# First attention stage: pooled projections first, separate operands for the pooled and convolved channels, two output chunks in each late step

## The reference, cut to what matters

```python
h = modulate(rmsnorm(x, g_mix), sh1, sc1)
proj = h @ w_in                       # q, k, v: 512 each; u_pool, b_gate, c_gate, x_conv: 256 each
attn = diff_attention(q, k, v, ...)   # 8 heads, two softmaxes each, over 512 x 512
y_a = rmsnorm(attn, g_subln) * 0.8                       # 512 channels
y_b = multiscale_pool(u_pool, w_pool, pool_scale)        # 256: window means less the token, a 64x64 map, a scale
y_c = b_gate * conv3(c_gate * x_conv)                    # 256
mixed = concatenate([y_a, y_b, y_c]) @ w_out
x = x + gt1 * mixed
```

## Time and profile before

| what | value |
|---|---|
| median of 3 runs | 1758.97 us |
| the profiled execution | 1761.21 us, its span 1759.4 us |
| TensorE matmul busy | 1699.7 us, 97% of the span |
| VectorE, ScalarE, GpSimd busy | 822.9, 618.2, 139.6 us |
| mean granted clock of TensorE | 0.984 |
| the 17 steps of the first attention | about 74.6 to 235.3 us |
| first addition to x of the attention's own output chunks | 258.33 us |

### The profile page before, as it was taken

One profiled execution on the slowest core, in us unless ns is written; L12 is line 12 of the kernel. 1 busy time (PEld: TensorE's weight loads), 2 busy tenths in 40 slices (PEclk: granted clock), 3 DMA queues, 4 the chain that ended last, 5 costly groups with the idle time before them and its releaser, 6 DMA issues.

```text
span 1759.4 us, 22619 instructions
## 1 busy us (share of the span) xinstructions
PE 1699.7 (97%) x7999; PEld 1367.6 (78%) x7999; DVE 822.9 (47%) x1272; ACT 618.2 (35%) x1071; POOL 139.6 (8%) x142
## 2 busy tenths in 40 slices
PE   5999998999999999999999999999999999999998
PEld 3866576888888888888888887677788888888886
DVE  4788756443333334444444434666455544444332
ACT  4365534222222323322222221555443322223222
POOL 0002101000001113000001030002001100000000
PEclk8999898999999999999999999999999999999998
DMA  9543113443333326333343346122233333333331
GB/s 344 194 133 114 42 54 94 141 131 95 95 100 99 98 85 151 95 95 95 95 118 99 94 126 116 50 59 70 72 95 95 90 99 98 96 95 109 99 98 64
DMA packets 296590, 184.55 MB, mean 105 GB/s; under 512 B 15051, under 2 KB 285895, under 8 KB 295495
## 3 DMA queue, kind: packets, MB, share of 16 engines
q1 hardware_dynamic: 290912, 169.89, 32.2%
q0 software_dynamic: 3968, 12.70, 3.0%
q10 hardware_dynamic: 1656, 1.25, 0.2%
HBM read 180.67 MB, written 6.36 MB: 106 GB/s over the span
## 4 chain that ended last, share of the span: by engine, by line
PE 91%; DVE 4%; ACT 1%; DMA 1%; issue 1%; SPq 0%; DVEq 0%; ACTq 0%
PE psum L546 28%; PE psum L548 28%; PE psum L547 28%; DMA ada_w<-in_w_ada 1%; PE psum L936 1%; PE psum L909 1%; DVE w_lo L1533 1%; PE psum L727 1%; PE psum L952 1%; DVE p L1633 1%; PE psum L687 1%; PE psum L703 0%; PE psum L782 0%; ACT w_hi L1120 0%; DVE acc L1526 0%
## 5 line engine op out<-in xcount | busy, mean ns | idle before, releaser
L546 PE MATMUL psum<-h_hi,w_hi 128*128 128x512 f32 x1480 | 588.6, 398 | 15.5 <-DVE w_lo L1533 5.6
L547 PE MATMUL psum<-h_lo,w_hi 128*128 128x512 f32 x1480 | 578.9, 391 | 0.0
L548 PE MATMUL psum<-h_hi,w_lo 128*128 128x512 f32 x1480 | 578.9, 391 | 0.0
L1533 DVE TENSOR_TENSOR w_lo<-w_raw,w_hi 128x1024 fp32r<-128x1024 f32 (+2 forms) x266 | 353.1, 1327 | 327.1 <-ACT w_hi L1120 322.5
L546 PEld LDWEIGHTS psum<-h_hi,w_hi 128*128 128x128 f32 x1480 | 279.3, 189 | 99.8 <-issue 26.0
L1120 ACT ACTIVATE w_hi<-w_raw 128x1024 fp32r<-128x1024 f32 (+2 forms) x266 | 288.4, 1084 | 151.7 <-PE psum L548 145.5
L548 PEld LDWEIGHTS psum<-h_hi,w_lo 128*128 128x128 f32 x1480 | 279.3, 189 | 59.8
L547 PEld LDWEIGHTS psum<-h_lo,w_hi 128*128 128x128 f32 x1480 | 279.6, 189 | 56.0 <-issue 0.5
L546 PE MATMUL psum<-hid_hi,w_hi 128*128 128x512 f32 x528 | 205.5, 389 | 0.0
L548 PE MATMUL psum<-hid_hi,w_lo 128*128 128x512 f32 x528 | 205.4, 389 | 0.0
L547 PE MATMUL psum<-hid_lo,w_hi 128*128 128x512 f32 x528 | 205.4, 389 | 0.0
(11 more groups left out here) (240 smaller groups left out, 1389.3 us busy)
## 6 DMA issues: line engine op xcount, KB each, us to landing
w_raw<-in_w_in SPq DMA_DIRECT2D x50, 512.0 KB, 3.8
w_raw<-in_w_gate_up SPq DMA_DIRECT2D x44, 512.0 KB, 3.7
w_raw<-in_ffn_w_gate SPq DMA_DIRECT2D x44, 512.0 KB, 3.7
w_raw<-in_ffn_w_up SPq DMA_DIRECT2D x44, 512.0 KB, 3.6
w_raw<-in_ffn_w_down SPq DMA_DIRECT2D x32, 704.0 KB, 4.4
sq<-in_w_ada SPq DMA_DIRECT2D x24, 512.0 KB, 4.8
w_raw<-in_w_down SPq DMA_DIRECT2D x16, 704.0 KB, 4.4
ada_w<-in_w_ada SPq DMA_DIRECT2D x8, 1024.0 KB, 17.4
```

What stands on the lines that cost most here:

```text
L546: pe.matmul(o, a_hi, b_hi, start=start, stop=False)
L547: pe.matmul(o, a_hi, b_lo, start=False, stop=False)
L548: return pe.matmul(o, a_lo, b_hi, start=False, stop=stop)
L1533: dve.tensor_tensor(w_lo[:, s % 2, 0:n], w_raw[:, s % 2, 0:n], w_hi[:, s % 2, 0:n].bitcast(F32), ALU.subtract).then_inc(w_ready, 1)
```

## The change

The order of the projections is changed: u of the channels 128 to 255 (u1) is first and u0 fourth, the convolution's slabs come one or more places later, and the last keys stand right before the step that reads them. The two products with `w_pool` go into steps 5 and 6, in bank 0. The side channels get buffers of their own (`side_hi`, and `side_lo` in the place of `y_side`), written as soon as each is known. Side chunks stand in pairs in steps 14, 15 and 16, in bank 7 and then banks 0 and 1, with two behind (bank 2 and 7). The semaphore counts `GEN` are renumbered.

```diff
+        at1 += -at1 % PAGE
         y_side = place("y_side", [P, 4, T], F32, at1)
+        side_lo = place("side_lo", [P, 4, T], F32R, at1)
...
+        POOL_STEP = {5: 1, 6: 0}
...
-        for n, b_ in enumerate((7, 0, 1, 2, 3, 7, 4, 5)):
+        for n, b_ in enumerate((7, 7, 7, 7, 0, 1, 2, 7)):
...
-        KINDS1 = [("cg", 0), ("q", 1), ("k", 1), ("xc", 0), ("cg", 1), ("q", 2), ("k", 2), ("xc", 1),
-                  ("u", 1), ("q", 3), ("k", 3), ("u", 0), ("bg", 0), ("bg", 1)]
+        KINDS1 = [("u", 1), ("q", 1), ("k", 1), ("u", 0), ("cg", 0), ("xc", 0), ("q", 2), ("k", 2),
+                  ("cg", 1), ("xc", 1), ("q", 3), ("k", 3), ("bg", 0), ("bg", 1)]
+        SIDES = [1, 0, 2, 3]
...
# TensorE, in step t
                 if t < N_MIX1:
                     part(S_MIX1 + t, 0, 2)
-                elif t == N_MIX1:
-                    pe.wait_ge(wpool_landed, 64)
-                    pe.wait_ge(pooled, 2)
-                    pool_product(0)
-                elif t == UN1:
-                    side_chunk(2)
+                else:
+                    side_chunk(2 * (t - N_MIX1))
...
+                if t in POOL_STEP:
+                    pe.wait_ge(wpool_landed, 64)
+                    pe.wait_ge(pooled, 2 - POOL_STEP[t])
+                    pool_product(POOL_STEP[t])
                 if t < N_MIX1:
                     part(S_MIX1 + t, 1, 2)
-                elif t == UN1 - 1:
-                    side_chunk(0)
-                    side_chunk(1)
...
+                else:
+                    side_chunk(2 * (t - N_MIX1) + 1)
...
# ScalarE
+            def side_high_of(c, done_by):
+                wait_emptied(act, done_by)
+                act.activation(side_hi[:, c, :], y_side[:, c, :], ACT.Identity).then_inc(side_high, 1)
...
                 if t < UN1:
                     exps(t, 1)
...
+                if t in POOL_STEP:
+                    keep_pool(POOL_STEP[t])
+                if t - 1 in POOL_STEP:
+                    side_high_of(POOL_STEP[t - 1], ("pool", POOL_STEP[t - 1]))
+                if t == N_MIX1 - 1:
+                    side_high_of(2, ("slab", S_MIX1 + KINDS1.index(("bg", 0))))
...
# VectorE
+            def side_low_of(c):
+
+                dve.wait_ge(side_high, SIDES.index(c) + 1)
+                dve.tensor_tensor(side_lo[:, c, :], y_side[:, c, :], side_hi[:, c, :].bitcast(F32), ALU.subtract)\
+                   .then_inc(side_ready, 1)
...
+                if t > N_MIX1:
+                    add_side(2 * (t - N_MIX1) - 1)
...
+                if t == N_MIX1:
+                    side_low_of(3)
...
-                if t <= N_MIX1:
+                if t < N_MIX1:
                     split_low(S_MIX1 + t + 1)
+                else:
+                    add_side(2 * (t - N_MIX1))
+                    split_low(S_SIDE + 2 * (t - N_MIX1) + 1)
+                    split_low(S_SIDE + 2 * (t - N_MIX1) + 2)
+                if t - 1 in POOL_STEP:
+                    side_low_of(POOL_STEP[t - 1])
+                if t == N_MIX1 - 1:
+                    side_low_of(2)
                 for r in range(KD, 3 * KD):
                     if step_of(r) == t:
                         mod_step(r)
```

More of the change, by code:

```diff
@@ L314, in program @@
         sub_added, sub_root = sem("sub_added"), sem("sub_root")
+        side_high, side_ready = sem("side_high"), sem("side_ready")
         pads_set, pooled, conved = sem("pads_set"), sem("pooled"), sem("conved")
@@ L381, in program @@
             plan_slab(("slab", s_), 7, s_)
-        for c in range(2):
-            plan(("pool", c), 7)
-        for n, b_ in enumerate((7, 0, 1, 2, 3, 7, 4, 5)):
+        for n, b_ in enumerate((7, 7, 7, 7, 0, 1, 2, 7)):
             plan_slab(("side", n), b_, S_SIDE + n)
@@ L660, in side_chunk @@
                 b = take(("side", n))
-                chunk(psum[:, b, :], S_SIDE + n, [2, 3, 0, 1], [hs[k] for k in (6, 7, 4, 5)], (h_ready, 8 * GEN["y"]))\
+                chunk(psum[:, b, :], S_SIDE + n, SIDES, [(side_hi[:, c, :], side_lo[:, c, :]) for c in SIDES],
+                      (side_ready, 0))\
                     .then_inc(w_used, 1)
@@ L753, in _ @@
                 b = take(("out1", n))
-                chunk(psum[:, b, :], S_OUT1 + n, range(4), hs[0:4], (h_ready, 8 * GEN["y"] + 4)).then_inc(w_used, 1)
+                chunk(psum[:, b, :], S_OUT1 + n, range(4), hs[0:4], (h_ready, GEN["y"])).then_inc(w_used, 1)
             def out_proj(key, s0, xs, js, ready):
@@ L796, in ffn @@
                 s0 = S_GU[f]
[L797 removed]
+                h0 = GEN[f"ffn{f}"]
                 def pair(n, i=None):
@@ L1217, in _ @@
                     split_high(S_MIX1 + t + 1)
-                if t == N_MIX1:
-                    split_high(S_SIDE + 1)
-                if t == UN1 - 1:
-                    keep_pool(1)
-                    for c in range(2):
-                        wait_emptied(act, ("pool", c))
-                        act.activation(h_hi[:, 4 + c, :], y_side[:, c, :], ACT.Identity).then_inc(h_high, 1)
-                if t == UN1:
-                    split_high(S_SIDE + 3)
+                if t >= N_MIX1:
+                    split_high(S_SIDE + 2 * (t - N_MIX1) + 1)
                 if t >= 3 and t % 2:
@@ L1242, in _ @@
                            .then_inc(emptied[b], 1)
-                if t == N_MIX1:
-                    keep_pool(0)
                 if t < UN1:
                     exps(t, 1)
-                if t == N_MIX1:
-                    act.wait_ge(w_used, S_SIDE)
-                    for c in range(2):
-                        wait_emptied(act, ("slab", S_MIX1 + KINDS1.index(("bg", c))))
-                    for c in (2, 3):
-                        act.activation(h_hi[:, 4 + c, :], y_side[:, c, :], ACT.Identity).then_inc(h_high, 1)
-                if t == UN1 - 1:
-                    split_high(S_SIDE + 2)
-            split_high(S_SIDE + 4)
+                if t in POOL_STEP:
[4 more added lines that the diff above has]
+                    side_high_of(2, ("slab", S_MIX1 + KINDS1.index(("bg", 0))))
+            split_high(S_SIDE + 7)
             keep_o1(UN1 // 2 - 1)
             square_o1(3)
-            split_high(S_SIDE + 5)
+            split_high(S_OUT1)
             wait_emptied(act, "sub_sum")
@@ L1644, in _ @@
                         mod_step(r)
-                if t == N_MIX1:
-                    for c in (2, 3):
-                        low(h_lo[:, 4 + c, :], y_side[:, c, :], h_hi[:, 4 + c, :], 6 + c)
-                elif t == UN1 - 1:
-                    for c in (0, 1):
-                        low(h_lo[:, 4 + c, :], y_side[:, c, :], h_hi[:, 4 + c, :], 10 + c)
-                    split_low(S_SIDE + 2)
-                elif t == UN1:
-                    split_low(S_SIDE + 3)
-                    add_side(1)
             dve.scalar_tensor_tensor(out=el[:, :], in0=lsum[:, 0, :], scalar=EPS, in1=lsum[:, 0, :],
                                      op0=ALU.mult, op1=ALU.mult).then_inc(sub_added, 1)
-            split_low(S_SIDE + 4)
-            add_side(2)
-            split_low(S_SIDE + 5)
-            add_side(3)
+            add_side(5)
+            split_low(S_SIDE + 7)
+            add_side(6)
+            split_low(S_OUT1)
             dve.wait_ge(sub_added, 1)
@@ L1668, in _ @@
             for c in range(4):
-                split_low(S_SIDE + 6 + c)
-                add_side(4 + c)
+                if c == 1:
+                    add_side(7)
+                    split_low(S_OUT1 + 1)
                 b = wait_filled(dve, ("sub", c))
@@ L1674, in _ @@
                 dve.wait_ge(y_set, c + 1)
-                low(h_lo[:, c, :], k1[:, c, :], h_hi[:, c, :], 12 + c)
+                low(h_lo[:, c, :], k1[:, c, :], h_hi[:, c, :], GEN["y"] + c)
             def col_of(name, n, i, step):
```

35 lines of the change are left out of this document (17 added, 18 removed).

## The result

The changed kernel takes 1764.18 us as the median of 20 runs (1758.57 to 1766.8), the kernel before 1758.85 us (20 runs). The ratio is 1.0026, with a 95% interval of 1.0019 to 1.0034: about 4.6 us slower (the two medians differ by 5.3). The forecast was 2.6 us slower, within 0.2%; the stated range of 1758.5 to 1765 held the time. The profiled execution took 1766.62 us. This is the head of its page: the span, and the busy times.

The account below looks back on a forecast made before the run. TensorE, busy in 97% of the span, was taken as the bound, so only its waits and clock could give time back. Terms of +3.8 up to step 14, +2.4 and -3.6 took 1759.0 to 1761.6 us; range 1755 to 1767, own 1758.5 to 1765.

Parts of the forecast that it names:

- One sign of being wrong: Behind the first out1 addition: any difference of more than 1 us would speak against the forecast.
- within 0.2%: Whole kernel: a change under 3.5 us counts as the same; given chance 0.46.
- Window sums in step 1: GpSimd's u1 sums slow VectorE by 4.0 us, TensorE waits before step 2's transposes; +4.7 us.
- wait plus clock: Step 2: 3.0 us of TensorE waiting plus 1.7 us for the halved clock, together +4.7 us.
- The same sums gone from step 9: Steps 10 and 11 shorten once the window sums leave step 9; -4.7 us.
- The convolution's products in step 10: Moved there, they make TensorE wait, +1.5 us, and the clock may fall, +0.5 us as a mean.
- -1.9: Steps 10 and 11 with the wait for the last keys: forecast difference in us.
- Step 14: With two side chunks inside, waits of 1.7 and 2.6 us and 1.7 for the clock: 16.7 us, +2.4.
- The tail: Step 15 to the first out1 addition: 38.6 us instead of 42.2, -3.6, set by the four-tile chain.
- (A): Clock stays low some 7 us behind the waits in steps 2 and 14: +7.1, 1766.1 us; chance 0.20.
- (B): Window sums in step 1 cost next to nothing: 1756.9 us, or 1755.2 with the clock up; chance 0.20.
- (C): Side chunks fill step 14 without waits: 10.4 us, -3.9 instead of +2.4, kernel 1755.3 us; chance 0.10.

Follow-up runs that it names:

- experiments 10 and 11: One kernel timed twice: the changed kernel with the moves of experiment 5, experiment 6 and experiment 7 and another projection order; ratios 0.9966 and 0.9963 to the kernel before.
- experiment 8: Changed kernel with useless matmuls filling TensorE's waits in steps 2 and 14; ratio 1.0029 to the kernel before, step 2 at 13.99 us.
- experiment 2: Kernel before with GpSimd's window sums left out, one short subtraction in their place; ratio 0.9984 to the kernel before.
- experiments 3: Kernel before with only the new projection order and the two w_pool products in steps 5 and 6, side chunks unmoved; ratio 1.0019.
- experiment 7: Changed kernel with the addition of side chunk 7 ahead of the four-tile chain and the second out1 slab's split behind it; ratio 1.0023 to the kernel before.
- experiment 9: Changed kernel with one modulation row instead of two in steps 1 and 9, one more in steps 6 and 14; ratio 1.0027 to the kernel before.
- those of 1: Changed kernel with GpSimd's window sums left out, one short subtraction in their place; ratio 1.0012 to the kernel before.
- experiment 5: Changed kernel with the low part of side tile 2 moved from the end of step 13 to the start of step 14; ratio 1.0015 to the kernel before.
- experiment 6: experiment 5 plus VectorE's weight split ahead of step 14's reductions and chunk 0's addition between them; ratio 1.0013 to the kernel before.

## Why the prediction came out as it did

**The sign, the places and the sum were right; the size was 2 us short in the medians.** In the profiles the stage lost 3.15 us where 2.6 was forecast. By the ratio it is 4.6. The difference is smaller than what single executions show on either side: the profiled run of the changed kernel lay 2.4 us above its median, that of before 2.3. Where the other 2 us of the medians are stays open. Much of the spread goes with the clock: of the 20 runs of the changed kernel the fastest four (1758.57 to 1760.62) had a mean granted clock of 0.987 or 0.988, the slowest four (from 1765.43) 0.983.

One sign of being wrong did show: behind the first `out1` addition the profile of the changed kernel is 1.97 us longer (1503.04 us for 1501.07), where more than 1 us was to speak against the forecast. That sign was set too narrow, since two profiles of one kernel, experiments 10 and 11, differ there by 5.2 us, with mean clocks of 0.989 and 0.987.

The result lies just outside "within 0.2%", which had the largest chance, and its interval reaches across that bound.

**Window sums in step 1: right size, half the mechanism.** +4.7 was forecast, +4.2 measured. The slowdown of VectorE by 4.0 us was right (4.35). The wait stood at another place, since I followed only the transposes and not the copy of `q` that frees bank 7 behind ScalarE's exponentials. And the sum "wait plus clock" is not what set the step: experiment 8 takes the clock's part away and the step stays. VectorE's loss alone, 4.35 us, gives the 4.2. That 3.0 of wait and 1.7 of clock came near it was luck.

**The same sums gone from step 9** brought 4.8 us in experiment 2 (4.7 forecast).

**The convolution's products in step 10: the mis-sized term.** I charged 0.5 us as the mean of clock up and clock down. The runs show no mean but two values. Steps 10 and 11 took 22.03 to 22.11 us in the profiles of the changed kernel and of experiments 3, 7 and 9, and 20.45 to 20.48 in those of 1, 5, 6 and 8. The wait is 1.48 or 1.49 us in all of these. After it the clock was 0.50 over 180 to 182 in the changed kernel and 1.00 in experiment 5:

```profile
180.00:182.00 2.00, 2.00 (x11) 0.50 (x9) 0.00 (x0) 0.38 (x1) 0.00 (x0) 0.50 0.37 143
```

```profile
180.00:182.00 2.00, 2.00 (x14) 1.18 (x7) 1.20 (x3) 0.04 (x1) 0.00 (x0) 1.00 0.35 137
```

Half level costs 1.6 us there. In the forecast the term was 0.5, in the profiled execution it came to 1.6, and that is nearly all of the way from -1.9 to -0.7.

**Step 14: right.** The waits were forecast as 1.7 and 2.6 and are 1.56 and 2.20; the clock's 1.7 came to 1.6 in this execution. It too is one of two values: beside the same waits the clock reads 0.57 in the changed kernel and 1.00 in experiment 9.

```profile
216.00:220.00 4.00, 4.00 (x12) 3.11 (x11) 0.29 (x1) 1.94 (x6) 0.00 (x0) 0.57 0.44 131
```

```profile
218.00:222.00 4.00, 3.53 (x19) 3.01 (x19) 2.74 (x4) 3.13 (x8) 0.00 (x0) 1.00 0.44 131
```

**The tail: right**, 38.9 us for 38.6, with the two instructions in the chain that the sum had counted (experiment 7).

**The rivals.** (A) falls: behind 2.19 us the clock was 0.52 over 93.5 to 97 and back at 1.00 from 98, so half level lasted 3.4 us and not 7; in step 14 the same (0.57 over 216 to 220). In the tail, where it wasn't looked for, the clock did stay low for longer, 0.50 over 257.5 to 264, and 0.79 there before; the first addition still came within 0.3 us of the forecast. (B) falls with step 2. (C) falls with the two waits of step 14; with them taken away (experiment 6) step 14 takes 13.0 us and not 10.4, since three waits of 0.6 to 0.75 us stay.

By the Trainium skill's rule of the shared pair of ports ("SBUF — State Buffer", "Who interferes with whom"), which the prediction weighed, whichever of VectorE and GpSimd comes second stands until the other's instruction is through. The trace of the changed kernel agrees, once single instructions are laid side by side:

```profile
86.64 1.30 POOL L1995 TENSOR_TENSOR pool_s<-pool_s 128x512 f32<-128x512 f32 x1
87.40 0.56 DVE L1580 TENSOR_SCALAR quad<-quad 128x2 f32<-128x2 f32 x1
...
89.24 1.21 DVE L1530 TENSOR_TENSOR w_lo<-w_raw,w_hi 128x1024 fp32r<-128x1024 f32 x1
89.38 2.20 POOL L2008 TENSOR_TENSOR rs<-pool_s,rs_fin 64x512 f32<-64x512 f32 x1
90.38 2.29 DVE L1523 SCALAR_TENSOR_TENSOR acc<-sq,cact,acc 128x1024 f32<-128x1024 f32 x1
```

The tiny instruction, begun while one of GpSimd's ran (to 87.94), ends at 87.96. The row ends 1.1 us behind GpSimd's instruction (92.67 and 91.58), and so does the second row (94.90 and 93.82), and both rows of the kernel before. `w_lo` began first and took its usual 1.21 us; there it was GpSimd's instruction that took 2.20 us, where its twin at 88.01 took 1.28. So a row lost the rest of the GpSimd instruction that it met, 1.0 and 0.85 us here, and the price of a whole one, 2.1 us, didn't come. That the prediction's time by that price, 1764.0, is near the 1764.18 measured is luck.

## What to carry to other kernels

A loss that two engines cause each other moves with the work; ask in which step the slowed engine has slack, and not in which step the other one is idle. In a step that several chains cross, a wait on the busiest engine is not the price of a cause: find the chain that reaches the step's last instruction, and look for a second one of nearly the same length before counting a gain. And a term that hangs on the clock after a short wait has two values in single profiles, not a mean: compare stretches between profiles only after sorting them by it. Before calling an instruction slow or unharmed beside another engine's, look which of the two began first.
